# A PEER layer on one Trainium2 core: every expert slot gathered as one row of u and one of v, without a joined table

## What is computed

```
def block(t):                                   # 128 tokens, 4 blocks
    q = (t @ wq).reshape(128, 8, 2, 128)
    s = einsum('tpcd,pckd->tpck', q, sub_keys)
    s1, i1 = top_k(s[:, :, 0], 16)
    s2, i2 = top_k(s[:, :, 1], 16)
    ...                                         # best 16 of the 256 pairs
    idx = ...                                   # (128, 8, 16): 128 experts of 16384 per token
    g = softmax(top)
    a = gelu(einsum('tpkd,td->tpk', u[idx], t))
    return einsum('tpk,tpkd->td', g * a, v[idx])
```

## Time and profile before

| | |
|---|---|
| median of 3 runs | 3413.37 us (3404.31 to 3429.4) |
| the profiled execution | 3420.92 us, span 3419.1 us |
| TensorE busy | 2701.8 us, 79% |
| VectorE busy | 2011.6 us, 59% |
| ScalarE busy | 1185.8 us, 35% |
| GpSimd busy | 840.8 us, 25% |
| HBM read, written | 841.70 MB, 136.31 MB |
| mean granted TensorE clock | 0.889 |

### The profile page before, as it was taken

One profiled execution on the slowest core, in us unless ns is written; L12 is line 12 of the kernel. 1 busy time (PEld: TensorE's weight loads), 2 busy tenths in 40 slices (PEclk: granted clock), 3 DMA queues, 4 the chain that ended last, 5 costly groups with the idle time before them and its releaser, 6 DMA issues. The chain is left out here.

```text
span 3419.1 us, 41254 instructions
## 1 busy us (share of the span) xinstructions
PE 2701.8 (79%) x15753; PEld 2241.9 (66%) x15753; DVE 2011.6 (59%) x3632; ACT 1185.8 (35%) x2151; POOL 840.8 (25%) x813
## 2 busy tenths in 40 slices
PE   6999768885555555555556679889999999899998
PEld 5887656674555545455545567667888777778886
DVE  3223574668766855784455545457875465678753
ACT  2111411345555555565556531242220102421201
POOL 0112442245444444444444412001000000110000
PEclk9999988997777787777777879989999999999999
DMA  8999979989999999999999952202333231023322
GB/s 284 300 297 281 289 245 280 292 318 419 421 421 421 420 421 421 416 416 421 421 420 418 421 210 92 68 1 92 96 94 93 80 117 56 7 87 98 97 88 80
DMA packets 158521, 848.26 MB, mean 248 GB/s; under 512 B 15824, under 2 KB 16080, under 8 KB 94736
## 3 DMA queue, kind: packets, MB, share of 16 engines
q0 software_dynamic: 113280, 680.83, 52.7%
q1 hardware_dynamic: 45072, 165.12, 14.5%
HBM read 841.70 MB, written 136.31 MB: 286 GB/s over the span
## 5 line engine op out<-in xcount | busy, mean ns | idle before, releaser
L195 PE MATMUL PS<-AR_r,RHI 128*128 128x512 f32 (+2 forms) x1912 | 753.9, 394 | 33.6 <-DVE RING_r L1638 7.1
L197 PE MATMUL PS<-AR_r,RING_r 128*128 128x512 f32 (+2 forms) x1912 | 748.5, 391 | 0.0
L944 PE MATMUL PS<-IDN,HL 128*128 128x128 f32 x2688 | 477.7, 347 | 340.2 <-ACT HL L1458 340.2
L1847 DVE SCALAR_TENSOR_TENSOR AR<-AR 128x1024 f32<-128x1024 f32 x410 | 501.5, 1224 | 398.7 <-DMA AR<-peer_uv,XC 358.3
L944 PEld LDWEIGHTS PS<-IDN,HL 128*128 128x128 f32 x2688 | 413.0, 181 | 404.9 <-ACT HL L1458 397.4
L196 PE MATMUL PS<-AR_r,RHI 128*128 128x512 f32 (+1 forms) x1688 | 659.2, 391 | 0.0
L573 POOL DMA_INDIRECT AR<-peer_uv,XC x398 | 455.9, 1145 | 540.0 <-ACT HL L1458 317.2
L1636 DVE CAST RHI<-RING 128x1024 fp32r<-128x1024 f32 x256 | 178.8, 698 | 450.0 <-DMA RING<-in_wstream 447.0
L195 PEld LDWEIGHTS PS<-AR_r,RHI 128*128 128x128 f32 x1912 | 366.2, 192 | 112.9 <-issue 20.8
L197 PEld LDWEIGHTS PS<-AR_r,RING_r 128*128 128x128 f32 x1912 | 365.4, 191 | 74.7
L944 PE MATMUL PS<-IDN,AR 128*128 128x128 f32 x1408 | 255.9, 353 | 198.0 <-ACT AR L1458 198.0
(11 more groups left out here) (374 smaller groups left out, 3563.8 us busy)
## 6 DMA issues: line engine op xcount, KB each, us to landing
RING<-in_wstream SPq DMA_DIRECT2D x304, 512.0 KB, 3.6
peer_uv<-in_peer_u POOLq DMA_DIRECT2D x64, 1024.0 KB, 11.1
peer_uv<-in_peer_v POOLq DMA_DIRECT2D x64, 1024.0 KB, 13.1
AR<-peer_uv,XC POOLq DMA_INDIRECT x398, 14.4
XL<-in_xl SPq DMA_DIRECT2D x1, 2048.0 KB, 7.7
AR<-in_strips POOLq DMA_DIRECT2D x1, 2048.0 KB, 7.8
out_x<-XL SPq DMA_DIRECT2D x4, 512.0 KB, 2.7
AR<-in_na_bias POOLq DMA_DIRECT2D x1, 1536.0 KB, 14.1
```

Source lines behind the costliest of these rows:

```text
L195: pe.matmul(out, sh, mh, start=start, stop=False)
L197: return pe.matmul(out, sl, mh, start=False, stop=stop)
L944: mm = pe.matmul(sum_bank(tt, k), scaled_row(n)[:, P * k:P * k + P], IDN[:], start=(j == 0 and k % 4 == 0), stop=(j == SLOTS - 1), is_tran ...
L1847: dve.scalar_tensor_tensor(u, u, 1.0, HT[:, n // SLOTS, :], ALU.mult, ALU.mult, accum_out=RAW[:, n:n + 1]).then_inc(dotted, 1)
```

## The change

PEER_UV and all its copies go, with the waits for them; so do `copies` and `copy_rows`. Each slot from 24 on is gathered as the early ones were: one 4-KB row of u and one of v per partition, by two instructions behind the one wait for a free buffer. The semaphore of a buffer counts 32 a slot instead of 16 or 32. The order on the other engines is the same as before. The core of the diff:

```diff
-        PEER_UV = nc.dram_tensor("peer_uv", (NKEYS * NKEYS, 2 * D), F32, kind="Internal").ap()
...
-        def copy_rows(pool, i):
-
-            rows, x = slice(COPY_ROWS * (i // 2), COPY_ROWS * (i // 2 + 1)), i % 2
-            pool.dma_start(PEER_UV[rows, D * x:D * x + D], t[("peer_u", "peer_v")[x]][rows]).then_inc(uv_copied[i % IN_FLIGHT], 16)
...
-            return row_landed[n % NROW], 16 * (n // NROW + 1 + min(n // NROW + 1, EARLY // NROW))
+            return row_landed[n % NROW], 32 * (n // NROW + 1)
...
-            copies(8, in_flight=1)
-            copies(4, in_flight=2)
...
-            copies(46, in_flight=3)
...
-                if i % 16 not in (3, 6, 9, 12, 15):
-                    copies(1)
...
-            copies(2, in_flight=2)
             for d in range(2):
                 pool.memset(NEAR[d], 0.0).then_inc(hg["zero"], 1)
...
-            copies(8, in_flight=2, after_chunk=iter(range(FIRST["mod2"] + 6, FIRST["mod3"] + 4, 3)))
-            copies(8, in_flight=2)
...
-            copies(6, in_flight=2)
...
-            add_seven(n2, "sq", SQUARES, behind=1)
+            add_seven(n2, "sq", SQUARES)
...
-            copies(10, in_flight=2)
...
                     if n == EARLY:
                         pool.wait_ge(chunk_used, FIRST["wq"] + 16)
                         pool.wait_ge(pk_s, 16)
-                        copies(COPIES)
-                        for x, s in enumerate(uv_copied):
-                            pool.wait_ge(s, 16 * len(range(x, COPIES, IN_FLIGHT)))
...
                     pick = bass.IndirectOffsetOnAxis(ap=IDX[:, n:n + 1], axis=0)
-                    if n < EARLY:
-                        for x, name in enumerate(("peer_u", "peer_v")):
-                            pool.indirect_dma_start(row(n)[:, D * x:D * x + D], None, t[name], pick
-                                                    ).then_inc(row_signal(n)[0], 16)
-                        copies(int(n % 3 == 2), in_flight=1)
-                    else:
-                        pool.indirect_dma_start(row(n), None, PEER_UV, pick).then_inc(row_signal(n)[0], 16)
+                    for x, name in enumerate(("peer_u", "peer_v")):
+                        pool.indirect_dma_start(row(n)[:, D * x:D * x + D], None, t[name], pick
+                                                ).then_inc(row_signal(n)[0], 16)
```

More of the change, by code:

```diff
@@ L11 @@
 from contextlib import ExitStack
-from itertools import islice
 import concourse.bass as bass
@@ L59 @@
 ADD_AT, SQUARE_AT, SUM_AT, ROOT_AT, SCALE_AT, LEAD_AT = (LAST + a for a in (24, 40, 56, 64, 72, 96))
-COPY_ROWS = 256
-COPIES, IN_FLIGHT = 2 * NKEYS * NKEYS // COPY_ROWS, 3
 SECTIONS = [("mod1", 16), ("q", 4), ("k", 4), ("v", 4), ("hq", 4), ("zf", 4), ("zb", 4), ("i", 4), ("g", 4),
@@ L383, in build @@
         pk_s, pk_sc, pk_top, pk_exp, pk_idx = (sem(f"pk_{k}") for k in ("s", "sc", "top", "exp", "idx"))
-        uv_copied = [sem(f"peer_uv_copied{j}") for j in range(IN_FLIGHT)]
         row_landed = [sem(f"row_landed{j}") for j in range(NROW)]
@@ L459, in _, with add_seven @@
             steps = Steps(pool, pool_step)
[L460 to L472, removed]
+            def add_seven(s, ready, x):
                 for k in range(KT - 1):
-                    copies(behind, in_flight=2)
                     after(pool, s, ready, k + 1, KT)
@@ L485, in _ @@
             passing(pool, 1)
-            pool.wait_ge(chunk_used, 1)
-            copies(8, in_flight=1)
-            copies(4, in_flight=2)
             pool.wait_ge(phase, 4 * 1)
```

## The result

The changed kernel takes 3488.02 us (median of 4 runs, 3460.82 to 3495.12) against 3421.39 us (4 runs, 3404.31 to 3429.5) of the kernel before on the same chip: a ratio of 1.0187, 95% interval 1.0114 to 1.0259. It is slower, by 67 us where the prediction said 167, and the time lies inside the range that it gave. The profiled execution took 3482.42 us, with a span of 3480.6 us where the earlier trace rows come from one of 3419.1.

The account below looks back on a forecast made before the run. The DMA engines were taken to bound the gathers at 2.49 us a slot, with GpSimd next. The terms: 3421 + 220 + 0 - 50 = 3591 us from the profiled execution, stated as 3580 us; range 3450 to 3670 us.

Parts of the forecast that it names:

- item 1: Gathers of slots 24 to 511: doubled issues make GpSimd the bound, 2.94 us a slot instead of 2.49, +220 us.
- (b): Pricing a gather slot by the mean issue of the kernel before: 2 x (1.145 + 0.30) = 2.89 us.
- (c): Pricing a gather slot with dot products falling evenly against issues, a hit waiting 0.61 us on average: 2.99 us.
- R1: Gathers: hits mostly miss, issue and dot product locked in phase; slot 2.56 to 2.7 us, 3405 to 3465 us; chance 0.12.
- the forecast: Main case for the gathers: a slot of 2.7 to 3.15 us, kernel 3465 to 3685 us; chance 0.76.
- Item 2: Gathers: same bytes in half-size rows, 2.60 us a slot at 404 GB/s, under GpSimd's 2.94 us, so no cost.
- Item 3: Table copies and GpSimd's waits for them gone, mostly ahead of slot 24: 50 us saved, ends 25 and 75.
- The stall of 17 us: At 400 us VectorE waits for buffers that GpSimd clears only after waiting for a copy; 17 us to be saved.
- Item 4: Each slot's second gather has no wait but still 0.30 us before it; VectorE waits once for both: nothing.
- R2: GpSimd keeps 2.49 us a slot and removing the copies gives more than 85 us: 3349 us; chance 0.05.
- R3: Gathers: GpSimd and VectorE hold each other up; slot 3.72 us, 3963 us, or in part 3700 to 3800; chance 0.07.
- The signs: Expected profile after: issues 1.10 to 1.25 us, DMA 340 to 380 GB/s, landings near 5 us, gather stretch 1390 to 1500 us.

## Why the prediction was right in direction and too large

**GpSimd as the bound, item 1: the mechanism right, the term mis-sized.** An issue costs the same for 4 KB as for 8, 0.94 us undisturbed and 0.30 behind it, and the hits by the two-input operation go straight into the slot: the PSUM runs show it.

The term was 488 x (2.94 - 2.49) = +220 us; it measured +136.9. The step that failed is the choice of one value between (b) and (c) for every slot, which rests on "if a dot product of 1.23 us a slot falls evenly against the issues" and a wait of 0.61 us on average. The number of hits was right: 435 of 976 issues, where 1.23 / 2.94 of them are 408. Their size was not: 0.25 us on average instead of 0.61, because 265 of them cost 0.055 us as in the locked phase; the other 170 cost 0.55 us each. Outside the lock a slot takes 2.92 us, close to the 2.94 forecast, but 24 of 60 groups of 8 slots are locked at 2.56. Where the slot reaches the rate of the DMA engines, the dot product comes to start 0.2 us behind an issue, and the next one is hit by 0.05 to 0.09 us only; how it is pulled there (I think by the landings) no run isolates.

Way (c) gives 2.99, 2.67 and 3.40 us for dot products of 1.22, 0.69 and 1.76 us; measured were 2.776, 2.616 and 3.53. So (c) is no law: it is too high for the two shorter ones and too low for the long one.

Rival R1 had this lock, at 0.12, and it holds for a part of the slots (2.61 to 2.67 us in slots 192 to 255 and 320 to 447); what I used against it ("no gap wider than 1.245 us for a 1.23-us operation") overlooked that the operation needs no gap, only to begin behind an issue. The other half of that argument, that the selection keeps the two from locking, fits the run without selection. And R1 was priced as a state of the whole run; what came is a mixture of it and the forecast. Way (b) took the mean of the kernel before, 1145 ns, over to both issues; they had 1127 and 1038.

**Item 2.** In the locked stretches the 4-KB rows set the pace, at 408 or 409 GB/s, close to the 404 that the weight chunks gave (2.60 us forecast, 2.56 measured). It cost nothing elsewhere, as said.

**Item 3, the copies: -50 forecast, -62.8 measured,** inside the ends of 25 and 75 but not made up as I had it. By points that both traces have, the gain stands at 6.0 us at the first split of a chunk (55.0 to 49.0), at 19.2 when the mixer's operations of the earlier trace rows begin (395.7 to 376.5), at 33.6 at the last modulation multiplication (533.3 to 499.7), at 49.7 at the first gather (653.0 to 603.3) and at 62.8 at slot 24. I had 7 before the mixer, 17 in it, 5 behind it and 21 in the early slots; it was 19, 14, 16 and 13. So the sentence that VectorE's waits for chunks "lie under a TensorE that is busy throughout and give nothing" was wrong for the projections: ahead of the mixer, where 12 us more came than I had counted, these waits fell from 185.3 to 167.5 us. Behind the mixer came 11 us more than I had counted, and there they fell only from 9.4 to 2.8 us, so where the rest of it comes from stays open; the early slots gave 8 less. The stall of 17 us has gone, as forecast.

**Item 4.** Right: 0.30 us before 1008 gathers.

**What the sum left out.** An emptier queue also ends sooner: the last row lands and is used 9.0 us after its issue, not 16.2, 7.2 us less. I had forecast the short landing and put its effect at nothing in the sum. The 5.4 us of the second block, which the change doesn't touch, I leave unexplained; the runs of either kernel differ by more.

**The rivals.** R2's early gain of 85 us did not come. R3 is refuted: 410 dot products of 1224 ns on average, before and after.

The Trainium skill, page "SBUF — State Buffer", section "SBUF: two separate sides", makes the shared port pair a lock under which either engine fully blocks the other; the runs bear out one direction only, GpSimd's gathers waiting for a two-input operation of VectorE. Of VectorE operations in a 2-port mode the same section says that GpSimd can't write descriptors meanwhile and the DMA engines sit idle; it does not say so of operations with two SBUF inputs. Here they have an effect of that kind: the share of the DMA engines falls to 0.87 and their rate to 298 GB/s with the long dot product, and they are 1.02 and 404 GB/s with the same one out of PSUM.

**The signs.** Right: about 1000 gathers with 0.30 us before them, 1.127 us for u, GpSimd busy 1264.9 us, no stall at 400; the landing, 6.4 us, came near the 5 or 6 given. Outside what I gave: the v gathers' mean of 1.038 (1.10 to 1.25 forecast), slot 24 at 710 (715 to 735), the gather stretch of 1352 us (1390 to 1500), and the DMA share, 0.97 to 1.00 where I had said below 0.95: at 361 GB/s the engines count as nearly full, so this share does not show a spare capacity of 12%, the rate does.

## What to carry to other kernels

When GpSimd issues the gathers, count its issues first: here each, of 128 rows, costs about 1.245 us whether a row has 4 or 8 KB, and as soon as two of them fill the slot, every overlap with a VectorE operation that has two inputs in SBUF is paid in full. Moving one operand of that operation to an idle bank of PSUM takes the overlap away at no cost to VectorE, and is worth nothing where GpSimd has slack (ratio 1.0018 in the kernel before, 90 us in the changed one). Overlaps of two periodic engines need not be random. Pricing them by an even spread fitted 36 of 60 groups of slots here (2.92 us against 2.94) and was 0.38 us a slot too dear in the other 24, so give the locked phase a share of the slots, and not only a chance of being the whole run.

## What I had not expected of the hardware

- The delay lasts until 0.81 to 0.83 us after the end of the two-input operation, the same with dot products of 1.23 and 1.76 us and with the added operation of 0.70 us, and with the issue's start nearly anywhere inside them. An operation of the same size with one of its inputs in PSUM delays none of 268 issues.
- Two inputs are not the only case: the cast of a weight chunk (line 1594, one input in SBUF, 128 x 1024) held both gathers of the changed kernel that started well inside it, to 1.46 and 1.13 us, and they too ended 0.82 us behind it. A handful of gathers a kernel meets one, so it weighs nothing here.
- Rows of 4 KB come at 408 to 409 GB/s and rows of 8 KB at 420 to 421, in gathers from random places: 3%, though the queue of GpSimd's transfers has 148,736 packets with two gathers a slot and 78,464 with one.
- One more small VectorE operation with its wait in each slot made ScalarE wait 131 us before its scalings into HL, where it had no wait in the changed kernel, and lengthened a slot by 0.2 us beyond all issuing. This was seen in four kernels and its cause stays open.
